# Side streams of a fused two-block layer placed by an account of engine times instead of fixed rates

## The reference

```python
# block 1
h = x + 0.5*rmsnorm(swiglu(rmsnorm(x)))                  # D_FF = 2816
z, xbc, dt, q, k, v, gates = split(rmsnorm(h) @ w_in)
xs, B, C = silu(causal_conv4(xbc))                       # 4 groups x 8 heads of 64, state 128
y_ssd = rmsnorm(ssd_chunked(xs, dt, A, B, C) * silu(z)) @ w_ssd        # 4 chunks of 128
y_att = rmsnorm((softmax(q1 k1) - lam*softmax(q2 k2)) v) @ w_da        # 8 heads, causal, ALiBi
h = h + rmsnorm((g0*y_ssd + g1*y_att) @ w_out)
h = h + 0.5*rmsnorm(swiglu(rmsnorm(h)))
# block 2
q, k, v = silu(causal_conv4(..)); q, k = l2norm(q), l2norm(k)          # 8 heads of 128
T = inverse(I + strict_lower(beta k k^T * decay))        # 8 chunks of 64, per head
o = scan over the chunks of (u = T v beta, w = T k beta decay)         # gated delta rule
mask = top_256(sum_h iw_h * relu(iq_h ik^T))             # indexer; ik = layernorm
o2 = softmax(q k^T masked) v                             # 8 heads, 2 key heads
h = h + (g0*o*silu(z) + g1*o2) @ w_out2
h = h + (silu(conv3(a)) * conv3(b)) @ w_down2;  out = rmsnorm(h)
```

## Time and profile before

| | |
|---|---|
| median of three runs | 2808.53 us (2806.12 to 2810.29) |
| the profiled execution's own time | 2809.54 us |
| its span in the profile | 2807.5 us |
| mean granted TensorE clock | 0.965 |
| busy: PE, DVE, ACT, POOL | 2609.6, 1547.2, 1128.1, 47.2 us |
| PE's share of the chain that ended last | 69% |

### The profile page before, as it was taken

The page is one execution under the profiler, slowest core; times in us unless marked ns, Lnnn a source line. Parts: engine busy times, 40 slices in busy tenths (PEclk is TensorE's granted clock), DMA queues, the critical chain, the costliest instruction groups (busy, mean ns, idle before and its releaser), DMA issues.

```text
span 2807.5 us, 33817 instructions
## 1 busy us (share of the span) xinstructions
PE 2609.6 (93%) x13762; PEld 2053.8 (73%) x13762; DVE 1547.2 (55%) x2406; ACT 1128.1 (40%) x1695; POOL 47.2 (2%) x44
## 2 busy tenths in 40 slices
PE   8999998898999999999999998988989997999998
PEld 6888876676776777777888875756667674888886
DVE  5444266656656665346444266677555445577742
ACT  4222244655435445544223235233424255444421
POOL 0000000000000000000000000000000000000000
PEclk9999999899999999999999999999999998999999
DMA  4333322121221122222323321111111110223332
GB/s 141 98 98 92 99 92 65 45 75 53 63 81 53 60 76 67 68 90 79 99 93 100 98 89 62 32 45 32 60 46 39 61 60 30 83 98 98 96 98 77
DMA packets 59193, 209.93 MB, mean 75 GB/s; under 512 B 6560, under 2 KB 6560, under 8 KB 59040
## 3 DMA queue, kind: packets, MB, share of 16 engines
q1 hardware_dynamic: 57600, 204.38, 22.9%
q10 hardware_dynamic: 1440, 3.41, 0.3%
HBM read 205.66 MB, written 2.10 MB: 74 GB/s over the span
## 4 chain that ended last, share of the span: by engine, by line
PE 69%; DVE 16%; ACT 12%; issue 3%; DMA 0%; DVEq 0%; SPq 0%; ACTq 0%
PE bank L1470 20%; PE bank L1471 19%; PE bank L1472 19%; ACT fB L1794 3%; ACT L1792 3%; DVE hl L2108 2%; ACT hl L1811 2%; PE bank L1672 2%; ACT fA L1794 2%; DVE fA L2236 2%; DVE fB L2236 1%; PE bank L1597 1%; DVE small L2405 1%; PE bank L1509 1%; PE bank L1485 1%
## 5 line engine op out<-in xcount | busy, mean ns | idle before, releaser
L1470 PE MATMUL bank<-uR,hl 128*128 128x512 f32 x2160 | 892.0, 413 | 26.1 <-DVE uR L2120 11.9
L1471 PE MATMUL bank<-uR,hl 128*128 128x512 f32 x2160 | 857.5, 397 | 0.0
L1472 PE MATMUL bank<-uR,hl 128*128 128x512 f32 x2160 | 856.7, 397 | 0.0
L2108 DVE TENSOR_TENSOR hl<-raw,hl 128x1024 fp32r<-128x1024 f32 (+1 forms) x391 | 472.7, 1210 | 540.9 <-ACT hl L1811 540.1
L1470 PEld LDWEIGHTS bank<-uR,hl 128*128 128x128 f32 x2160 | 415.0, 192 | 149.7 <-issue 46.8
L1811 ACT CAST hl<-raw 128x1024 fp32r<-128x1024 f32 (+1 forms) x391 | 401.7, 1030 | 259.2 <-PE bank L1472 248.3
L1472 PEld LDWEIGHTS bank<-uR,hl 128*128 128x128 f32 x2160 | 414.3, 192 | 90.2
L1471 PEld LDWEIGHTS bank<-uR,hl 128*128 128x128 f32 x2160 | 415.4, 192 | 84.3 <-issue 5.0
L1470 PE MATMUL bank<-act,hl 128*128 128x512 f32 x528 | 206.9, 392 | 0.0
L1471 PE MATMUL bank<-act,hl 128*128 128x512 f32 x528 | 205.7, 390 | 0.0
L1472 PE MATMUL bank<-act,hl 128*128 128x512 f32 x528 | 205.7, 390 | 0.0
(11 more groups left out here) (460 smaller groups left out, 2736.6 us busy)
## 6 DMA issues: line engine op xcount, KB each, us to landing
raw<-in_win SPq DMA_DIRECT2D x147, 512.0 KB, 3.5
raw<-in_w SPq DMA_DIRECT2D x44, 512.0 KB, 3.5
raw<-in_w1g SPq DMA_DIRECT2D x22, 512.0 KB, 3.5
raw<-in_w1u SPq DMA_DIRECT2D x22, 512.0 KB, 3.5
raw<-in_w2g SPq DMA_DIRECT2D x22, 512.0 KB, 3.5
raw<-in_w2u SPq DMA_DIRECT2D x22, 512.0 KB, 3.5
raw<-in_w1d SPq DMA_DIRECT2D x16, 512.0 KB, 3.5
raw<-in_wssd SPq DMA_DIRECT2D x16, 512.0 KB, 3.6
```

What stands on the lines that cost most here:

```text
L1470: e.matmul(s.bank[:, :], h[:, 0, w], hi, start=s.first and q == 0, stop=False)
L1471: e.matmul(s.bank[:, :], h[:, 0, w], lo, start=False, stop=False)
L1472: i = e.matmul(s.bank[:, :], h[:, 1, w], hi, start=False, stop=s.last and q == n - 1)
L2108: e.tensor_tensor(h[:, 1, 0:s.width], x[:, 0:s.width], h[:, 0, 0:s.width].bitcast(F), ALU.subtract).then_inc(*sig("dve_split.lo", s))
```

## The change

`RATES`, `NW` and `LAG` go. Each step that is added to `plan` is entered in an account: `costs` gives for its kind the engines and durations in order (measured constants, some in proportion to the tile's width), `spend` moves four clocks, one for each engine, and notes when each of its signals comes. A side stream asks `ready` for what it needs before it adds a step: its inputs and PSUM banks are there by the account when TensorE's clock has come that far, and neither DVE's nor ACT's clock is more than `AHEAD` = 3.0 us ahead of TensorE's. `schedule` takes a step of the first side stream that has one ready, and a piece of the main stream only when none has; when all hold, TensorE's clock is moved on by 0.25 us.

```diff
+def costs(s):
+    if k == "mm":
+        return [("PE", 0.68 * len(s["xs"]), "pe_gemm.mm")]
+    if k == "split":
+        return [("ACT", 1.0, "act_split.hi"), ("DVE", 1.2, "dve_split.lo")]
+    if k == "conv":
+        return [("ACT", 0.7), ("DVE", 0.78 * (s["taps"] - 1), "dve_conv.tap", s["taps"] - 1)]
...
+    return COSTS.get(k, ())
...
+    def spend(s):
+        t = max((when(x) for x in s.values()), default=0.0)
...
+        for engine, us, *name in costs(s):
+            t = clock[engine] = max(clock[engine], t + 0.06) + us
+            if name:
+                at[(name[0], s.id, name[1] if len(name) > 1 else 0)] = t
+
+    def ready(*xs, banks=0):
+        def now():
+            if len(SB.left) < banks:
+                return False
+            t = max(when(list(xs)), when([y for _, after in SB.left[:banks] for y in after]))
+            return t <= clock["PE"] and max(clock["DVE"], clock["ACT"]) <= clock["PE"] + AHEAD
+        while not now():
+            yield HOLD
...
     def schedule(main, sides):
...
+            for side in list(sides):
+                r = next(side, END)
+                if r is END:
+                    sides.remove(side)
+                if r is not HOLD:
+                    moved = True
+                    break
+            if not moved and going:
                 r = next(main, END)
                 going = r is not END
-                moved = r is not HOLD and going
...
+            if not moved:
+                clock["PE"] += 0.25
```

```diff
-        for n in range(T4 + lb):
+        for n in range(T4 + 1):
             if n < T4:
-                P[n] = front(n)
...
+                P[n] = yield from front(n)
+            if n:
+                yield from ready(P[n - 1][0], banks=1)
+                A[n - 1] = pv_turn(c, P[n - 1][0], P[n - 1][1], n - 1)
+            if n < T4:
+                yield from soft(P[n])
+            if n:
+                yield from ready(A[n - 1], V, banks=1)
+                tpv = pv_mul(A[n - 1], n - 1, V, o)
             yield
```

```diff
+    def prep_side():
         yield from narrow_side()
         for p, hs in enumerate(PAIRS):
-            yield from until(lambda: "v" in S[hs[1]])
+            yield from until(lambda: "v" in S[hs[1]] and (p < 2 or "o" in S[2 * p - 4]))
             yield from gdn_prep(p, hs)
+
+    def scan_side():
+        for p, hs in enumerate(PAIRS):
+            yield from until(lambda: "w" in S[hs[1]])
             yield from gdn_scan(p, hs)
             yield from gdn_out(p, hs)
...
-             [(gdn_side(), RATES[2]), (index_side(), RATES[3])])
+             [scan_side(), prep_side(), index_side()])
```

```diff
-ORDER1 = "t g0 g1 z0 r8 g2 b0 z1 r8 g3 b1 z2 r8 a0 a1 b2 z3 r8 a2 a3 c4 b3 c5 c6 c7 E F"
-ORDER2 = "n p0 x z0 h0 p1 z1 h1 p2 z2 h2 p3 z3 h3 k d0 d1"
+ORDER1 = "t g0 g1 z0 r8 z1 b0 g2 r8 z2 b1 g3 r8 a0 a1 b2 z3 r8 a2 a3 c4 b3 c5 c6 c7 E F"
+ORDER2 = "n p0 x p1 z0 h0 p2 z1 h1 p3 z2 k z3 d0 d1"
-TABLES = {ACT.Ln: "natural_log_exp_and_others", ACT.Exp: "natural_log_exp_and_others",
-          ACT.Silu: "silu_and_others", ACT.Tanh: "silu_and_others", ACT.Sigmoid: "sigmoid_and_others"}
-NB1, NB2, NA = 24, 24, 11
+TABLES = {ACT.Ln: ("natural_log_exp_and_others",), ACT.Exp: ("natural_log_exp_and_others", "exp_and_others"),
+          ACT.Silu: ("silu_and_others",), ACT.Tanh: ("silu_and_others", "exp_and_others"), ACT.Sigmoid: ("silu_and_others",)}
+NB1, NB2, NA = 24, 27, 11
```

More of the change, by code:

```diff
@@ L269, in step, with when @@
         plan.append(s)
+        spend(s)
         return s
+    clock = dict.fromkeys(("PE", "ACT", "DVE", "POOL"), 0.0)
+    at = {}
+    def when(x):
+        if isinstance(x, Page):
+            return when(x.t)
+        if isinstance(x, list):
+            return max((when(y) for y in x), default=0.0)
+        if not isinstance(x, tuple) or not isinstance(x[0], str) or x[1] is None:
+            return 0.0
+        return at.get((x[0], x[1]["id"], x[2] if len(x) > 2 else 0), 0.0)
+    def spend(s):
+        t = max((when(x) for x in s.values()), default=0.0)
+        t = max([t] + [when(x.after) for x in s.values() if isinstance(x, Page) and x.pool in (MB, SB)])
+        if s.kind == "mm":
+            t = max([t, when(("dve_split.lo", splits[s.j]))] + [when(ready) for hi, lo, ready in s.xs])
+        if s.kind == "split" and s.j - NHL in ends:
+            t = max(t, when(("pe_gemm.mm", *ends[s.j - NHL])))
+        for engine, us, *name in costs(s):
[10 more added lines that the diff above has]
+            yield HOLD
     par_in, con_in = ("par_in", None, 16), [("con1_in", None, 16), ("con2_in", None, 16)]
@@ L363, in group_rstd @@
         qs[2].release(("pool_norm.sum4", s2, 2))
-        for _ in range(NW[2] + 2):
-            yield
+        yield from ready(("pool_norm.sum4", s2, 2), banks=1)
         r = rstd([(qs[0][:, :], [("pool_norm.sum4", s2, 2)])], which)
@@ L585, in schedule @@
         END = object()
-        sides = [[x, rate, 0.0] for x, rate in sides]
-        going = True
+        sides, going, still = list(sides), True, 0
+        start = max(clock.values())
+        clock.update({x: start for x in clock})
         while going or sides:
             moved = False
-            if going:
+            for side in list(sides):
[6 more added lines that the diff above has]
+            if not moved and going:
                 r = next(main, END)
                 going = r is not END
-                moved = r is not HOLD and going
[L594 to L609, removed]
+                moved = r is not HOLD
+            still = 0 if moved else still + 1
+            if not moved:
+                clock["PE"] += 0.25
+            assert still < 400, "streams hold each other"
     def drop_pages(nb, rp, held):
@@ L672, in decay_side @@
         a.release(("dve_ssd.scan", s))
-        for _ in range(NW[1]):
-            yield
+        yield from ready(("dve_ssd.scan", s), banks=1)
         b = SB.take()
@@ L726, in ssd_core @@
         yield
+        yield from ready(*Xd[:3])
         xds = [fp.take() for _ in range(3)]
@@ L914, in front @@
         def front(i):
+            yield from ready(q, k, banks=2)
             n = slot["k"] % 4
@@ L1044, in narrow_side @@
         g_.release(("dve_gdn.nar", s))
-        for _ in range(NW[0]):
-            yield
+        yield from ready(nar, banks=4)
         bs, b, b3 = [SB.take(), SB.take()], SB.take(), SB.take()
@@ L1098, in gdn_prep @@
         yield from both(l2(k[0], 1.0, k2, 0), l2(k[1], 1.0, k2, 1), l2(q[0], DSC), l2(q[1], DSC))
-        for _ in range(NW[3]):
-            yield
+        yield from ready(nar, ("act_gdn.cols", cols, 1), banks=1)
         gb, gm = SB.take(), fp.take()
@@ L1112, in gdn_prep @@
         H.update(att=gm)
-        for _ in range(NW[4]):
-            yield
+        yield from ready(k2, banks=2)
         bs, kbe, kd = [SB.take() for _ in range(2)], [gp.take() for _ in range(2)], [fp.take() for _ in range(2)]
@@ L1187, in gdn_scan @@
         for c in range(C8):
+            if c:
+                yield from ready(("dve_gdn.state", before, 1), ("dve_gdn.state", before, 0), *w, banks=1)
             b = SB.take() if c else None
@@ L1208, in gdn_out @@
         o = S[hs[0]]["o"]
+        yield from ready(*o)
         qs = [fp.take() for _ in range(2)]
@@ L1338, in index_side @@
         yield from until(lambda: iq[3] is not None and "cols" in S2)
+        x = ikp[0]
+        yield from ready(x, banks=1)
+        b = SB.take()
+        s = step("ik_mean", x=x, xt=list(x.t), b=b)
+        x.t = [("dve_idx.mean", s)]
+        b.release(*x.t)
+        r = yield from side_rstd([(x[:, :], x.t)], O128)
+        yield from ready(r)
+        s = step("ik_norm", x=x, r=r)
+        x.t = [("dve_idx.ik", s)]
+        r.release(*x.t)
         yield from both(indexer(1), indexer(2))
```

281 lines of the change are left out of this document (198 added, 83 removed).

## The result

The changed kernel takes 2759.81 us in the median of four runs (2756.95 to 2765.34), beside 2808.87 us for the kernel before (2806.12 to 2810.29): a ratio of 0.983, 95% interval 0.981 to 0.985, 49 us faster. 2665 was forecast, 144 us faster.

The account below looks back on a forecast made before the run. TensorE was taken as the bound, with 148.9 us idle and 87 us of clock loss within reach. Idle 91 back, clock 58 back, `b0` hold 5 lost: 144 off 2809.5 gives 2665.5, stated as 2665; range 2600 to 2775.

Parts of the forecast that it names:

- The account in place of rates: Side steps of all three stages come when their input is made; if the account were true, all 236 us return.
- The prediction's sign of being wrong: More short waits keeping idle over 100 us, or one stage missing main matmuls for tens of us.
- What the account leaves out, 58 us: Stages A to C: 97 unbooked ACT table loads, each leaving TensorE waiting 0.6 us; bounds nothing to 124 us.
- The clock, two thirds of 87 us: Stages A to C: 58 of 87 us lost to TensorE's lower clock come back; bounds 0 and 87.
- The hold at `b0`, 5 us: Stage A: ten panels before `b0` instead of twelve, so main may hold; 5 us lost, at most 10.9.
- SSD groups at 75 to 90 us: Stage A: an SSD group, 109 us before, was expected to take 75 to 90.
- Cuts and outputs: Fronts, softmax and outputs cut in two: 0 beyond the sum, up to some us gained in `merge1` behind stage A.
- Scan beside preparation: Stage B: one pair's scan beside the next's preparation shortens the chain from 492 to 320 us, no longer the bound.
- Stage C: Changed profile should show no stretch of 20 us free of main matmuls in this stage.
- Half of it: Rival: unbooked ACT work takes 124 us as new 1.3 us waits, half the clock returns; 2741 us, chance 0.20.
- The full queue: Rival: DVE and ACT booked 3.0 us ahead slow stage A's 128 SSD steps; slower, 2845 us at 4.8 us a step, chance 0.09.
- No change: Rival: the account places steps no better than the rates, as real times scatter as much; 2809 us, chance 0.03.

Follow-up runs that it names:

- the fastest version: Changed kernel, with the account also booking the Silu after convolutions (stage A) and GpSimd's sum's wait for its squares, plus 1 us per hand-over in stage C: 2712.45 us (0.966).

## Why the prediction was off

The direction held; the time lies inside the range, but only a third of the gain came.

*What bounds the kernel.* Held: the same matmuls ran, and TensorE's idle time and clock are what moved.

*The account in place of rates: "if the account were true".* This is the step that failed. The forecast compared the account's constants with the rows, found them close, and took the rest as small delays. It did not ask which signals `when` can't find. A missing price makes a step late by that price; a missing link makes its result ready at time 0, and the reader is sent at once however far back the maker is. Stage A had ten waits of over 4 us where there were two; with two links mended it has four. The size was measured: the two links that were mended, the Silu and the sum, are 36 us of stage A. With the 1 us added in stage C, the fastest version recovers 47 of the 95 us by which the forecast missed; what the other 47 are is open. Of the idle time 91 us were to come back; 21.5 did (151.0 to 129.5), 34.8 and 3.6 in B and C less 16.9 in A. The prediction's sign of being wrong, idle time over 100 us, came; but with fewer and longer waits (37 became 31 in stage A), not with more short ones as it expected.

*What the account leaves out, 58 us.* Mis-sized as well as misread. Priced as waits of 0.6 us for 97 loads, it was measured by booking: the loads alone are worth 7 us in A and 5 in C, the Silu 17 in A, the sum 19 in A. Booking loads and Silu everywhere loses 12, since holds grow. The loads are 53, 24 and 14 in the three main streams, 91 beside the 97 forecast; cut in the same way the kernel before has 62, 26 and 14. They are 1283 ns each. The Trainium skill, "ScalarE: Activation LUTs", section "What ACT_TABLE_LOAD costs", adds a drain of 1380 ns to each; the trace of the changed kernel disagrees here as in the earlier trace rows: load at 744.49, the Silu at 745.79. No load of this trace has more than 12 ns between its end and ACT's next operation.

*The clock, two thirds of 87 us.* 29 us came back: by the windows 0.05 x 740 + 0.06 x 543 + 0.11 x 161 = 87 before, 0.06 x 767 + 0.01 x 480 + 0.05 x 152 = 58 after. That the clock follows the waits held stage by stage: B's loss is nearly gone (0.99), A's grew with its waits. The size was wrong as the idle was.

*The hold at `b0`, 5 us.* The number fits by luck, and the hold was mis-sized: it is 18.7 us long. Putting the order back brought 4.5 us, but the hold grew with it, from 18.7 to 23.4 us. It comes with the account, with 10.7 us of idle time in it and a clock of 0.71.

*SSD groups at 75 to 90 us.* Wrong: the first and the fourth group start at 461.2 and 779.0, 106 us a group against 109. So it wasn't the rates that set a group's pace. What does, its own chain of engines or the main panels that feed it, no run separates.

*Cuts and outputs.* Priced at nothing, some us expected in the merges: 7.6 us there, and little elsewhere.

*Scan beside preparation.* Held, and it carries the result: 62.5 us idle became 27.7, under the 30 forecast, and the clock 0.99. The chain from the first pair's norms at 1759.48 to the last pair's output at 2186.70 is 427 us, from 492; 320 was the estimate, on the condition that a step costs no more latency than before. That condition failed: beside each other both chains are slower. From a pair's norms to the last product of its preparation it is 107 and 103 us for the second and third pair (55 and 48 before), and 87 and 83 us for the first two scans (57 and 47 before). The 29 us that 1 us more a hand-over costs show the chain is still near the bound.

*Stage C.* Forecast to have no 20 us free of main matmuls: it has 20.8, and 10 us were gained. With 1 us more at each hand-over 8 more come.

*The rivals.* "Half of it" (2741) came nearest, by another mechanism than it named: not 1.3 us for each load, but a few links without a time. The full queue was not tested by itself; 106 us a group, no longer than before, speaks against it. "No change" was refused by a thin argument: that table loads always take 1283 ns says nothing of the signals that the account can't find.

## What to carry to other kernels

When an order is planned from a cost account, look first for results that the account holds ready at time 0 and for engines whose booked clock stands still, and only then at the constants: two missing links cost 36 us here, and a slack added behind one of them did nothing. Look also for where the planned order holds its main stream: TensorE's list of waits doesn't show the 49 us in which only side work ran; the gap between two main matmuls does. Read the gain by stage: the same edit (1 us more a hand-over) shortened two stages and lengthened the one whose chain is its bound. Two chains side by side and an order that knows when their steps are ready were worth 21 and 2 us of stage B alone, 63 together.

## What the runs showed of the hardware

Nothing unexpected in durations. Of the clock: stage B had 62.5 us idle and 0.94, then 27.7 us idle and 0.99, so a stage's mean came back almost whole when its waits shrank to single ones of 5 us at most, while stage A, with waits up to 7.8 us, stayed at 0.94. With the same order and the same 27.7 us idle a second trace of stage B shows 0.98 and 485.7 us, so a stage's clock scatters by about 0.01. In the fastest version the low clock of stage A lies where main matmuls are missing: 0.57 in the 48.7 us in front of `b0` (TensorE busy for 30.0 of them), 0.97 and 0.98 in the rest of the stage:

```profile
421.70:521.00 99.30, 93.92 (x415) 74.87 (x413) 64.99 (x92) 47.75 (x69) 0.00 (x0) 0.97 0.26 84
...
569.70:1152.50 582.80, 550.33 (x2587) 415.48 (x2587) 354.26 (x621) 289.41 (x499) 16.44 (x11) 0.98 0.21 66
```
